# Level products of the gated recurrence in visits of two levels

## What is computed

```python
def step(state, xs):                                   # one chunk of 64 tokens, 4 heads of 64
    qc, kc, vc, lfc = xs
    b = jnp.cumsum(lfc, axis=2)
    decay = jnp.where(causal, jnp.exp(b[:, :, :, None, :] - b[:, :, None, :, :]), 0.0)
    a = jnp.einsum('bhtd,bhsd,bhtsd->bhts', qc, kc, decay)
    o = jnp.einsum('bhts,bhse->bhte', a, vc) + jnp.einsum('bhtd,bhde->bhte', qc * jnp.exp(b), state)
    ...
```

## Time and profile before

| | |
|---|---|
| Median of three runs | 697.31 us |
| The profiled execution | 697.47 us, its span 695.6 us |
| PE busy | 687.8 us, 4036 matmuls |
| DVE busy | 463.7 us |
| ACT busy | 358.8 us |
| DMA, one panel | 1024 KB, 4.8 us from issue to landing |
| L1941, the level products | 448 matmuls in 7 visits |

### The profile page before, as it was taken

One profiled execution on the slowest core, in us unless ns is written; L12 is line 12 of the kernel. 1 busy time (PEld: TensorE's weight loads), 2 busy tenths in 40 slices (PEclk: granted clock), 3 DMA queues, 4 the chain that ended last, 5 costly groups with the idle time before them and its releaser, 6 DMA issues.

```text
span 695.6 us, 9973 instructions
## 1 busy us (share of the span) xinstructions
PE 687.8 (99%) x4036; PEld 554.7 (80%) x4036; DVE 463.7 (67%) x695; ACT 358.8 (52%) x561; POOL 12.4 (2%) x19
## 2 busy tenths in 40 slices
PE   9999999999999999999999999999999999999997
PEld 7889888877666668888887888788887888888886
DVE  5599964467767662283779556874669659729744
ACT  6856543655757663356555343544545443254651
POOL 1100000000000000003000000000000000000000
PEclk9999999999999999999999999999999999999999
DMA  9924333330211006513113421134113123313012
GB/s 330 368 80 174 123 122 122 123 128 16 70 60 61 1 26 244 245 61 121 61 60 123 165 77 61 60 122 182 60 61 122 61 91 121 117 65 121 13 63 108
DMA packets 15422, 76.40 MB, mean 110 GB/s; under 512 B 2000, under 2 KB 4080, under 8 KB 7824
## 3 DMA queue, kind: packets, MB, share of 16 engines
q1 hardware_dynamic: 14976, 72.92, 29.1%
q0 software_dynamic: 256, 2.84, 1.1%
q10 hardware_dynamic: 144, 0.00, 0.0%
HBM read 72.61 MB, written 2.10 MB: 107 GB/s over the span
## 4 chain that ended last, share of the span: by engine, by line
PE 91%; DVE 3%; ACT 2%; issue 2%; DMA 1%; SPq 0%; DVEq 0%; ACTq 0%
PE bank L1805 27%; PE bank L1806 26%; PE bank L1807 26%; PE bank L2141 2%; PE bank L2004 2%; PE bank L2153 2%; PE bank L1890 1%; PE bank L1941 1%; DMA raw<-wst 1%; ACT Whi L771 1%; DVE arena L1773 1%; PE bank L2029 1%; PE bank L1982 1%; PE bank L2157 0%; PE bank L2114 0%
## 5 line engine op out<-in xcount | busy, mean ns | idle before, releaser
L1805 PE MATMUL bank<-Xhi,Whi 128*128 128x512 f32 (+1 forms) x480 | 187.2, 390 | 0.7 <-DVE Xlo L1339 0.4
L1807 PE MATMUL bank<-Xhi,Wlo 128*128 128x512 f32 (+1 forms) x480 | 185.3, 386 | 0.0
L1806 PE MATMUL bank<-Xlo,Whi 128*128 128x512 f32 (+1 forms) x480 | 185.3, 386 | 0.0
L1805 PE MATMUL bank<-Whi,Uhi 128*128 128x512 f32 x272 | 106.9, 393 | 1.7 <-DVE Wlo L1209 1.6
L1805 PEld LDWEIGHTS bank<-Xhi,Whi 128*128 128x128 f32 x480 | 90.2, 188 | 20.9 <-DVE Wlo L1217 1.3
L1806 PE MATMUL bank<-Wlo,Uhi 128*128 128x512 f32 x272 | 105.9, 389 | 0.0
L1807 PE MATMUL bank<-Whi,Ulo 128*128 128x512 f32 x272 | 105.9, 389 | 0.0
L1807 PEld LDWEIGHTS bank<-Xhi,Wlo 128*128 128x128 f32 x480 | 90.2, 188 | 18.5
L1806 PEld LDWEIGHTS bank<-Xlo,Whi 128*128 128x128 f32 x480 | 90.2, 188 | 17.2
L771 ACT ACTIVATE Whi<-raw 128x2048 fp32r<-128x2048 f32 x27 | 51.7, 1914 | 56.1 <-PE bank L1807 51.6
L1217 DVE TENSOR_TENSOR Wlo<-arena,Whi 128x2048 fp32r<-128x2048 f32 x20 | 45.7, 2287 | 51.0 <-ACT Whi L779 51.0
(11 more groups left out here) (252 smaller groups left out, 915.5 us busy)
## 6 DMA issues: line engine op xcount, KB each, us to landing
raw<-wst SPq DMA_DIRECT2D x42, 1024.0 KB, 4.8
arena<-wst SPq DMA_DIRECT2D x16, 1024.0 KB, 4.8
arena<-ctab POOLq DMA_DIRECT2D x1, 2624.0 KB, 10.0
arena<-xt SPq DMA_DIRECT2D x8, 256.0 KB, 6.7
arena<-xn SPq DMA_DIRECT2D x4, 512.0 KB, 10.7
arena<-xn SPq DMA_DIRECT2D x1, 2048.0 KB, 7.8
out<-arena SPq DMA_DIRECT2D x7, 256.0 KB, 2.0
arena<-gpost SPq DMA_DIRECT2D x2, 512.0 KB, 7.3
```

The lines of the kernel that those rows point to most:

```text
L1805: mm(out_ap, w[0], x[0], start=start, stop=False, **kw)
L1806: mm(out_ap, w[0], x[1], start=False, stop=False, **kw)
L1807: return mm(out_ap, w[1], x[0], start=False, stop=stop, **kw)
```

## The change

The visits stand behind panels 3, 5, 7 (two levels each) and 8 (the last level). The steps `("level", n)` stand at panel 2 (n = 2), 3 (3), 5 (4 and 5) and 7 (6). The instructions themselves, their waits and their shapes are the same. `level` stands in the list where it stood, behind the split and before `gates` and `state_decay`; where there are two, they follow each other.

```diff
--- before.py
+++ after.py
@@ -443,7 +443,8 @@
         jobs_by = [sum(1 for j in jobs if j[0] <= g) for g in range(N_IN)]
 
 
-        LEVEL_AT = {g: g - 2 for g in range(2, 9)}
+        LEVELS_AT = {3: (0, 1), 5: (2, 3), 7: (4, 5), 8: (6,)}
+        PRODUCTS_AT = {2: (2,), 3: (3,), 5: (4, 5), 7: (6,)}
         STATE = 7
         steps = [("scale0",), ("split", 1), ("norm0",)]
         for g in range(14):
@@ -452,8 +453,8 @@
                 steps.append(("level_start",))
             if g == 2:
                 steps.append(("split", g + 2))
-            if g in LEVEL_AT:
-                steps.append(("level_mm", LEVEL_AT[g]))
+            for lev in LEVELS_AT.get(g, ()):
+                steps.append(("level_mm", lev))
             if g == 8:
                 steps.append(("state_turn",))
             if g == 9:
@@ -473,8 +474,8 @@
                 steps.append(("hg_norm",))
             if g == 0:
                 steps.append(("decay",))
-            if g in LEVEL_AT and LEVEL_AT[g] + 2 <= 6:
-                steps.append(("level", LEVEL_AT[g] + 2))
+            for lev in PRODUCTS_AT.get(g, ()):
+                steps.append(("level", lev))
             if g == 5:
                 steps.append(("gates",))
             if g == 7:
```

## The result

The kernel after takes 699.84 us in the median of 18 runs (698.21 to 700.85), the kernel before 698.09 in 18 runs beside it (697.02 to 699.46). The ratio is 1.0021, 95% interval 1.0012 to 1.0029: slower by 1.5 us. The forecast was slower by 1.1, with 697.31 as the time before.

The account below looks back on a forecast made before the run. The prediction took PE as the bound: 1.05 us saved in passages, but a 2.2 us wait for DVE at `state_turn`, net 1.13 us late. From 697.31 it forecast 698.4 us, range 697.0 to 699.6.

Parts of the forecast that it names:

- The saving of a joined visit: On PE, seven visits become four; each joined visit saves its 0.35 us passage in and out, 1.05 us in all.
- a joined level saves nothing: Rival: on PE the second level of a visit costs the full 1.29 us, giving 698.8 us; chance 0.13.
- DVE's chain: DVE's work from 66.41 us on, summed with new idle times: L1384 starts at 96.10 instead of 94.50, 1.6 us late.
- The three idle times: New DVE waits: 1.43 us before panel 5's second `scale_rows`, 0.5 before level 2's evacuation, 1.2 before level 5's products.
- Both thin covers on ACT: ACT's second sigmoid and split 8's high part finish 0.1 to 0.3 us before DVE wants them.
- The wait at `state_turn`: PE arrives at 97.56, stands 2.2 us for DVE's L1388 and starts L1951 at about 99.74.
- Passed on whole: Behind the wait PE's list has no slack, so its 1.13 us of lateness goes onto the end.
- no stall: Rival: PE does not stand at `state_turn`, only the saved passages count, 696.3 us; chance 0.12.
- The clock: Rival: PE's clock falls in the stall at `state_turn`, costing 2.4 us more, 700.8 us; chance 0.05.
- no change that can be told: Outcome for the whole kernel: a time within 0.2% (1.4 us) of before, 695.9 to 698.7 us; chance 0.68.

Follow-up runs that it names:

- c_state_early: b_five_at_6 with level 6 and the arguments of the state's decay moved ahead of panel 9's split; ratio to before 0.9984.
- a_fill: The kernel after with nine dummy products on PE filling its wait at `state_turn`; ratio to before 1.0017.
- h: h_after_halved: the kernel after with the 48 scores of 64 x 32 cut into two halves, panel steps between; ratio to before 1.0025.
- g: The kernel before with the 48 scores of 64 x 32 cut into two halves, two panel steps between; ratio to before 0.9995.
- b_five_at_6: The kernel after with level 5's step moved from panel 5 to panel 6, behind split 8; ratio to before 1.0007.
- i: The kernel after with the 48 scores halved and nine dummy products filling the wait at `state_turn`; ratio to before 1.0013.
- j: c_state_early with the 48 scores cut into two halves; median 696.70 us, ratio to before 0.9980.
- l: b_five_at_6 with the 48 scores cut into two halves; ratio to before 1.0007.

## Why the prediction was right, and where it was not

- *The saving of a joined visit.* 0.35 each was forecast, 1.05 in all. The seam costs nothing (2.02 us for two levels), and c_state_early is 1.0 us faster with a wait of 0.18 left. Right. The rival "a joined level saves nothing" is out, by the trace and by c. The trace of the weight loads (PEld) shows the passages: ahead of the visits they stand still for 2.3 us in 7 places before and for 1.3 in 4 after, waiting for no other engine.
- *DVE's chain.* The three idle times were forecast as 1.43, 0.5 and 1.2 and measured as 1.29, 0.43 and 1.13; L1384's start as 96.10, measured 96.14. Both thin covers on ACT held: the second sigmoid ended at 85.2 and DVE's product followed at 85.46.
- *The wait at `state_turn`.* Forecast 2.2 us with a start at 99.74; measured 2.04 and 99.77. The difference in length is the arrival: I took PE's own slot behind the visit (97.56), the record ends at 97.72.
- *Passed on whole.* Forecast +1.13; the lower groups give 698.36 - 697.37 = 1.0, and a_fill 1.0 on one chip. (Within the groups on one chip, h over g gives 0.8.) The rival "no stall" is out. It is however what c_state_early makes of the kernel, all but 0.18 us.
- *The clock.* The forecast put this term at nothing; that was wrong, though the number came out. The rival had a chance of 0.05 and a price of 2.4 us. A fall came in 11 of 18 runs, some of them probably by the thin stretch, and the two groups of after are 1.9 us apart. The price was too high because it took 4.9 us at half pace where the trace has 3.5. The argument against the rival was that 1.6 us of standing at 255 us had left the clock alone "and 2.2 us is not much more". At `state_turn` 2.0 us brought falls in six of twelve runs and 1.4 us in none of eleven. The Trainium skill (TensorE: Matmul & The Clock Gate, "HAM oscillation — how this bites in real kernels") describes such falls behind waits that are longer than this one. Here a wait of 2.04 us had the same effect, so the page would not have forecast it, and the measurement decides.
- *What the reference time means.* I took 697.31 as the kernel's time. It was the lower of two groups; 31 of 91 runs of before are in the upper. The profile of before couldn't show it, since it is one execution without a fall. So 698.4 was a forecast for the lower group, and after has 698.36 there. The median of all its runs, 699.84, lies above the range (699.6); only set against the 698.09 beside it, +0.21%, does it come to 698.8 on the old reference and into the range. That is partly luck: of the 1.5 us, 1.0 is the delay that was forecast, and the falls, which it left out, can make up the rest, 11/18 x 1.9 - 8/18 x 1.6 = 0.5. These shares rest on counts of few runs. 698.8 is also what "nothing saved" gave, so the time alone would not have decided between the two. Nor was it "no change that can be told": the interval lies clear of 1.

## What to carry to other kernels

Fewer, longer visits on the bound engine save their passages, but they bunch the work of the engine that feeds them: add up that engine's list to the next place where the bound engine waits for it, and count each round trip to a third engine that loses its cover. Three passages of 0.35 us here were paid with a wait of 2.0 us. Putting level 5 back under a split and one split (2.2 us) into the last round trip turned the loss into the gain. Look at the times of all runs and their mean clock before comparing medians of a kernel bound by TensorE.

## What the runs showed of the hardware that was not expected

- TensorE's clock fell behind a stretch in which it never stood still: 48 products of 64 x 32 in 2.9 us, each reading as busy (b_five_at_6, 155.7 to 158.6 us). With the stretch cut into two pieces of 1.5 us and six wide products between, none of the 45 runs of g, i, j and l has a fall (31 of 91 of the kernel before have one). Busy time is thus no sign that the clock is safe.
- A single wait of 2.0 us brought it down in half of the executions of one program (h, six of twelve), and a wait of 1.6 us at another place in none of 45. Whether a given execution falls looks like chance from outside; why is open.
- One fall costs 1.3 to 2.0 us here, the distance of the two groups in the kernels with several runs in both: the products run at half pace for about 3.5 us, and PE has no slack to take it up. In the kernel after this was from 100.6 to 104.1 us, with 0.85 us at full pace right behind the wait; in h_after_halved it began with the first product behind the wait (granted clock 0.50 from 99.8 to 103.1 us).
